# New costs in the table that lays three fronts' steps over the expert slots of a hybrid encoder layer

## What is computed

```python
u = rmsnorm(h, mix_norm)                       # 1024 x 1024
proj = u @ w_in                                # split in three head groups
y_a = windowed attention, 8 heads, 2 kv heads, window of 2 chunks of 64, sinks, ALiBi
y_b = Mamba-2: causal conv (4 taps) over 1536 channels, SiLU, chunked scan, 16 heads, SiLU gate
y_c = chunked attention, 8 heads, own chunk + 8 previous ones, learned relative bias
h = h + concat(rmsnorm of each) @ w_out
# PEER: per token 8 heads x 16 best of 128x128 product keys = 128 experts of one neuron each
q = rmsnorm(h) @ w_query;  scores against 2 x 128 sub keys;  top 16 of each, top 16 of the 256 sums
act = gelu(dot(un_t, peer_u[idx])) * gate      # 128 rows of 4 KB gathered for each token
h = h + sum(act * peer_v[idx])                 # 128 more rows of 4 KB for each token
h = h + sigmoid(rmsnorm(h) @ w_gate) * (p @ w_proj)
```

## Time and profile before

| | us |
|---|---|
| median of 3 runs | 3539.94 |
| lowest, highest | 3529.70, 3548.85 |
| profiled execution, its own time | 3562.65 |
| its span, first to last instruction | 3560.9 |

### The profile page before, as it was taken

One profiled execution on the slowest core, in us unless ns is written; L12 is line 12 of the kernel. 1 busy time (PEld: TensorE's weight loads), 2 busy tenths in 40 slices (PEclk: granted clock), 3 DMA queues, 4 the chain that ended last, 5 costly groups with the idle time before them and its releaser, 6 DMA issues.

```text
span 3560.9 us, 33937 instructions
## 1 busy us (share of the span) xinstructions
PE 2523.5 (71%) x11010; PEld 1225.6 (34%) x11010; DVE 2185.6 (61%) x5295; ACT 822.6 (23%) x2009; POOL 1959.4 (55%) x2064
## 2 busy tenths in 40 slices
PE   8998887767789777757768767758755555655446
PEld 5754454332344444322333445323321111111111
DVE  1346876666556866675655776685657666576640
ACT  3432333222133232130222222221211111111100
POOL 0002565565566655665656655665666666666664
PEclk9899897878889877878889876868876766677677
DMA  5436998889999998999999999999999999999996
GB/s 181 153 126 266 377 402 342 311 332 377 396 404 421 419 369 307 399 346 416 420 370 421 396 348 327 378 351 404 420 389 419 381 378 382 367 375 364 376 371 252
DMA packets 332294, 1267.09 MB, mean 356 GB/s; under 512 B 37288, under 2 KB 43600, under 8 KB 313432
## 3 DMA queue, kind: packets, MB, share of 16 engines
q0 software_dynamic: 294912, 1073.87, 77.5%
q1 hardware_dynamic: 37208, 191.04, 13.6%
HBM read 1256.22 MB, written 12.09 MB: 356 GB/s over the span
## 4 chain that ended last, share of the span: by engine, by line
PE 27%; POOL 16%; DVE 14%; another core or an unknown queue 14%; issue 14%; DMA 11%; ACT 3%; POOLq 0%; DVEq 0%; ACTq 0%
DMA v_ring<-peer_v,idx_v 8%; POOL v_ring L935 7%; POOL u_ring L921 6%; PE ps L1901 6%; DVE u_ring L1710 6%; PE ps L2172 6%; PE ps L2094 3%; PE ps L2105 3%; PE ps L2020 2%; DMA u_ring<-peer_u,idx_u 2%; PE ps L1988 1%; POOL front L921 1%; POOL front L935 1%; DMA front<-peer_u,idx_u 1%
## 5 line engine op out<-in xcount | busy, mean ns | idle before, releaser
L1710 DVE CUSTOM_DVE_ANT_0 u_ring<-u_ring,ps 128x1024 f32<-128x1024 f32 x928 | 1113.3, 1217 | 440.5 <-DMA u_ring<-peer_u,idx_u 351.6
L935 POOL DMA_INDIRECT v_ring<-peer_v,idx_v x912 | 869.1, 953 | 837.9 <-PE ps L2172 375.0
L921 POOL DMA_INDIRECT u_ring<-peer_u,idx_u x928 | 888.1, 957 | 639.1 <-DVE idx_u L1682 304.2
L2172 PE MATMUL ps<-v_ring,spread 128*32 128x512 f32 x3648 | 669.1, 828 | 554.8 <-DMA v_ring<-peer_v,idx_v 433.9
L1901 PE MATMUL ps<-front 128*128 128x512 f32 x1024 | 465.3, 610 | 13.9 <-ACT front L1199 8.0
L2172 PEld LDWEIGHTS ps<-v_ring,spread 128*32 128x32 f32 x3648 | 133.9, 134 | 905.6 <-issue 903.3
L1901 PEld LDWEIGHTS ps<-front 128*128 128x128 f32 x1024 | 196.3, 195 | 275.4 <-issue 275.1
L2105 PE MATMUL ps<-front 128*128 128x512 f32 x512 | 229.9, 604 | 3.2 <-issue 2.5
L2020 PE MATMUL ps<-front 128*128 128x256 f32 x768 | 190.4, 401 | 8.6 <-issue 8.1
L2172 PE MATMUL ps<-front,spread 128*32 128x512 f32 x448 | 102.2, 877 | 108.3 <-DMA front<-peer_v,idx_v 64.4
L2020 PEld LDWEIGHTS ps<-front 128*128 128x128 f32 x768 | 150.9, 202 | 51.1 <-issue 30.0
(11 more groups left out here) (264 smaller groups left out, 3062.6 us busy)
## 6 DMA issues: line engine op xcount, KB each, us to landing
front<-weight_blocks SPq DMA_DIRECT2D x140, 1024.0 KB
u_ring<-peer_u,idx_u POOLq DMA_INDIRECT x928
v_ring<-peer_v,idx_v POOLq DMA_INDIRECT x912
front<-x SPq DMA_DIRECT2D x14, 512.0 KB
front<-c_bias_all SPq DMA_DIRECT2D x32, 192.0 KB
front<-keys_turned SPq DMA_DIRECT2D x4, 1024.0 KB
front<-ple_w_gate SPq DMA_DIRECT2D x1, 4096.0 KB
out<-front SPq DMA_DIRECT2D x7, 512.0 KB
```

The lines of the kernel that those rows point to most:

```text
L921: nc.gpsimd.indirect_dma_start(row, None, io["peer_u"][0], bass.IndirectOffsetOnAxis(ap=k.idx_u[:, t % 2, j:j + 1], axis=0)).then_inc(here ...
L935: nc.gpsimd.indirect_dma_start(row, None, io["peer_v"][0], bass.IndirectOffsetOnAxis(ap=k.idx_v[:, m % 2, column:column + 1], axis=0)).the ...
L1710: nc.vector.tensor_tensor_reduce(out=row, in0=row, in1=k.un_ps, scale=1.0, scalar=0.0, op0=ALU.mult, op1=ALU.add, accum_out=k.dots[:, t % ...
L2172: last = mm(k.acc_ps[32 * j:32 * j + 32, half * 512:(half + 1) * 512], centres[:, at:at + 32], row[:, half * 512:(half + 1) * 512], start= ...
```

## The change

The table `PACE` gets other numbers. Nothing else is edited: every step, every instruction of it and every wait stays, in the same order within a front; the slots at which the steps of fronts 1 to 3 stand, and through them the rotation of the PSUM banks, are what differs.

```diff
-PACE = dict(n1=9.0, n1_t=1.2, p=4.7, a_k=0.7, a_turn=1.2, c_turn=1.2, a_s=0.9, a_t=1.2, a_v=0.9, c_s=1.2, c_u=1.2, c_v=0.9, x=3.7,
-            dt=1.8, cs=0.4, z=4.7, y_n=9.0, b_seg=1.4, b_turn=1.2, b_cb=1.0, b_off=4.0, b_diag=3.5, b_state=0.6, y_t=1.2, b_n=12.0, o=4.7, n2=10.0,
-            n2_t=1.2, q_t=1.2, q_s=1.2)
+PACE = dict(n1=9.0, n1_t=1.2, p=7.5, p_sum=2.0, root=4.0, a_k=0.7, a_turn=1.2, c_turn=1.2, a_s=4.2, a_t=1.0, a_v=0.7, a_o=4.0, c_s=3.0,
+            c_u=1.0, c_v=0.8, c_o=3.5, x=1.5, x_conv=5.4, dt=1.8, dt_soft=2.5, cs=0.4, z=7.5, y_n=8.0, b_seg=1.4, b_turn=5.0, b_cb=1.6,
+            b_off=14.7, b_diag=3.0, b_state=2.6, z_gate=4.5, y_t=1.4, b_n=10.0, o=7.5, n2=14.0, n2_t=1.2, q_t=1.2, q_s=1.2)
```

## The result

The changed kernel takes 3603.09 us (median of four runs, 3586.61 to 3611.20) beside 3544.39 us for the kernel before: ratio 1.0163, 95% interval 1.0131 to 1.0195. On a second chip it was 1.0184 (1.0116 to 1.0251). It is slower, by more than the range allowed. (The 3539.94 us given ahead of the prediction is the median of the first three of these four runs before.) Two executions far outside the others, one of `again` at 4734 us and one of the kernel before on the same chip at 5714 us, are in none of the ratios.

What follows compares the result with a forecast made beforehand. No engine full; a slot costs at least 2.48 us (POOL issues, gathers), and POOL's lost time, mostly on PE's values, is never regained. Front 1 +3.7, fronts 2 and 3 +2.0 each: +8 on 3539.94, 3548 us; range 3505 to 3590.

Steps and rivals of the forecast that it cites:

- the scan's term: Scan in fronts 1 to 3: 1.28 us a slot; 8, 11 and 11 more slots add +10.2, +14.1, +14.1 us.
- The bound above: Scan's upper limit: 2.48 us for each of the 30 added slots, +36 us.
- Conv 2.2: Conv stage: 2.2 us a slot; 6, 8 and 8 more slots add +13.3, +17.8, +17.8 us.
- Output 2.24: Output with n2: 2.24 us a slot; 3, 4 and 4 fewer slots give -6.7, -9.0, -9.0 us.
- Queries: Queries stage, five slots fewer per front: 1.0 us a slot in fronts 2 and 3, -5 each; front 1 -2.7.
- Chunk attention 1.0: Chunk attention: 1.0 us a slot; 3, 6 and 6 fewer slots give -3, -6, -6 us.
- The other three stages: Projections, y_n with z, and gates: fewer slots at POOL's 2.48 us each, -7.4, -9.9, -9.9 us.
- The parts costed at nothing: Step places inside stages, DVE and ACT waits, PSUM rotation: no term; x_conv's place up to +29 us a front if uncovered.
- 1 (scan under 120 us): Scan stops stalling because b_off steps stand further apart: -35 us, 3513 us; chance 0.28.
- 2 (chunk attention stays at 143 or more): Chunk attention and queries, which lose slots, don't shrink: +15 and +9 us, 3572 us; chance 0.17.
- 3 (clock): Scan's clock falls from 0.79 to 0.69, PE's 71 us grow by 10, three times: 3578 us; chance 0.07.
- 4: All stages: every slot costs the same, so moving slots changes nothing, 3540 us; chance 0.13.

Runs made afterwards that it cites:

- again: The changed kernel run once more, against the kernel before on the same second chip: ratio 1.0184.
- outer: Kernel before with each stage given about the changed kernel's slots, steps inside stages spread by old costs: 1.0135; on a faster chip 1.0098.
- after_scan_back: Changed kernel with the scan's 30 extra slots taken away and 28 of them given to chunk attention: ratio 1.0027 to the kernel before.
- plain: The kernel before, unedited, run and traced once more: ratio 1.0006, traced execution 3535.26 us.
- shift: Kernel before with all three fronts one slot later, costs unchanged: ratio 1.0002.
- chunk_for_conv: Kernel before with 11 slots moved from conv to chunk attention, costs inside stages as before: 0.9935; repeated on a faster chip (chunk_for_conv_c) 0.9977.
- inner_conv: Kernel before, stages keeping their slots, only the conv stage's steps spread by the new costs: ratio 1.0009.
- scan_light: Kernel before, old slots, with the VectorE operations of each b_off in fronts 1 to 3 cut to one head in eight: ratio 0.9988.
- changed_c: The changed kernel on a faster chip, against the kernel before on that chip: ratio 1.0062.
- inner: Kernel before with stages keeping about their old slots, steps inside every stage spread by the new costs: ratio 1.0085.
- inner_rest: Kernel before with new costs inside all stages but conv and scan with gates, slots about as before: ratio 1.0032.

## Why the prediction was wrong

The change's signs came out for every stage that the prediction took from the earlier trace rows, but the way in which it got the scan's price was unsound, and a part costed at nothing was not nothing.

**The step that failed** is the scan's term: 1.28 us a slot, "7.65 / 6", +38.4 us. Measured, a slot more in the scan costs 2.4 us on kind A (2.1 to 3.0 by which traces are compared, and more by `outer`) and 2.4 to 2.6 on kind B (1.5 by the pair with `after_scan_back`, which stays open). For the 30 slots that is +64 to +90 us. The price was taken from front 1 against fronts 2 and 3 in one trace. On kind A that difference drowns in what a stage varies by: the same division gives 1.28 in the first trace, -0.5 in *plain*, -1.9 in `shift` and 2.0 in `chunk_for_conv`, all with 27 and 33 slots. On kind B, where the stages repeat, it gives 0.9 in `inner_conv` and 1.1 in `chunk_for_conv_c`, and moving slots costs 2.5. So a second trace alone would not have saved it: front 1 against fronts 2 and 3 is no measurement of a slot's price in the scan. I noted that the result met the pace of slots without a front, 2.87 us, and took it for support; a stage's average pace says nothing of what one slot more costs.

The bound above was too low as well. It had 2.48 us for each slot, the least that POOL's two issues take, while the earlier trace rows already had 2.88 for a slot with no front beside it.

Why a whole slot: scan ran near the gathers' limit in *plain* (394 and 389 GB/s) and on kind B (409 and 405), and `scan_light` shows on kind B that its own VectorE work was not what the kernel waited for. In the first trace its rate was 366 and 363, so for kind A this reading rests on the trace and on the measured price.

**The base.** The +8 was laid on the median as if the 22.7 us by which the profiled execution was longer lay evenly. Against *plain* the first trace is longer by 19 us in scan, 14 in chunk attention and 8 in queries, and shorter by 6 each in conv and output. It was not the odd one in scan, though: `shift` and `chunk_for_conv` have 330 us there too. The forecast lengths after the change were better than their differences: scan 126 (130.3 and 134.7), chunk attention 139 (134.1, 132.8), output 102 (104.7, 107.8), queries 90 (85.3, 88.0), conv 152 (156.6, 164.4).

**The other terms.** Conv 2.2 a slot: 2.7 measured on both kinds, above POOL's 2.48; why was not tested. Output 2.24: right, 2.4 by *plain* and 1.8 on kind B (317.7 us in `inner_conv`, 297.6 in `changed_c`). Queries: 2.0 to 2.1 a slot on kind A and 3.0 on kind B. Fronts 2 and 3 stay within the bounds that I gave them; front 1 does not. I had called it bound by PE, with -2.7 us and a bound on the upper side only, and its five slots gave back 15 us (84.8 in *plain*, 70.0 after). Chunk attention 1.0: by the two traces after, 1.6 and 2.7. The other three stages: 11 slots gave back 9 to 10 us, not 27, on kind A, and 18 on kind B (514.0 in `changed_c`, 532.1 in `scan_light`).

**The parts costed at nothing.** The places inside the stages were given none, and `inner` measured +30 us on kind A, about half of the miss, though with a few slots moved between stages as said above; on kind B `inner_rest` is +11 us. That the scan's places have little part in it was measured on kind A, that conv's have little on kind B; what makes the rest was not isolated.

**The rivals.** 1 (scan under 120 us): no, 130 and more. 2 (chunk attention stays at 143 or more): no, 124 to 134. 3 (clock): scan's granted clock is 0.75 and 0.72 against 0.75 and 0.78 in *plain*; its PE work grew from 65 to 68 us to 76 to 85, of which the values of 11 slots account for some 9 (0.81 a slot by the earlier trace rows). How much of the rest is the clock was not isolated. 4: no, since moving slots did move the time; but on kind B it is nearer than I gave it credit for, with 2.4 to 3.0 us a slot in conv, scan and queries. None of them was what happened: the two stages that won slots, conv and scan, had no use for them.

The chip matters as much. The miss is 51 and 57 us on the chips of the first two comparisons and 12 us on kind B, where 20 us against 8 would have lain inside the range. That would have been luck: the scan's term is as wrong there (+73 us against +38), and queries, which gave back 45 us instead of 13, make up for it.

## What to carry to other kernels

Before giving a stage more room, ask whether it is waited for: in this kernel a stage that already ran near the gathers' rate paid the full price of each slot added, however busy its own engines looked. Shrink the suspected work and keep the schedule (`scan_light`); that asks directly, where comparing unlike stages does not. Don't build a term of 38 us on a difference of 8 us in one trace: take several traces of the unchanged kernel first. One more is not enough to tell which of two is the odd one, as the scan of *plain* shows. And price a slot by moving slots, not by comparing stages of different fronts.

## What the runs showed of the hardware

I had not expected that chips differ by 6 to 7% on one program: 3322 against 3544 us. In the slots with no front, gathers of 4 KB rows moved 374 GB/s on one chip and 419 on the other, with the engines' instructions alike; in weight-heavy stretches both reach 420. In these slots the traces' records of 4 KB packets have 168 ns on the mean on the first (*plain*), with 1.8% of them over 300 ns and the longest at 2.1 us, and 159 ns on the other (*changed_c*), with 0.07% over 300 ns and none over 0.5 us. The cause was not tested.

The Trainium skill ("HBM Reference", section "Specifications (TRN2)") gives about 358 GB/s a core when both cores of a pair stream, and some 425 for one alone. By it a busy neighbour is one reading of the two kinds; no run here shows that, and the rates of both kinds lie above its lower figure.
